# Bias rows built pair by pair on VectorE, two feature blocks side by side at the start of four layers, and fixed matmuls in nine waits of TensorE

## What is computed

```python
def first_block(...):                      # rows 0..271
    for i in range(2):
        a = rmsnorm(h, norm_mix_pre[i])
        m = forgetting_attention(a, ...) if i == 0 else gated_deltanet(a, ...)
        h = h + rmsnorm(m, norm_mix_post[i])
        f = conv_ffn(rmsnorm(h, norm_ffn_pre[i]), ...)
        h = h + rmsnorm(f, norm_ffn_post[i])
def second_block(...):                     # rows 16..271
    for layer in range(2):                 # MLA attention, then MoBA attention
        x = layer_norm(ALPHA * x + mixer(x, ...), ln_g[layer], ln_b[layer])
```

```python
logf = log_sigmoid(fl + b_forget); c = cumsum(logf, axis=1)
s = (q @ k.T) * 64 ** -0.5 + c_i[..., :, None] - c[:, :, None, :]
```

## Time and profile before

| | |
|---|---|
| time, median of 3 | 1306.91 us (1306.11 to 1307.09) |
| profiled execution, its own time | 1306.81 us |
| its span, first to last instruction | 1304.4 us |
| around the span | 2.4 us |
| busy: PE, DVE, ACT, POOL | 1198.2, 885.0, 714.1, 71.2 us |
| chain that ended last | PE 87%, DVE 7%, ACT 4%, issue 1% |
| mean granted clock of TensorE | 0.958 |

### The profile page before, as it was taken

One profiled execution on the slowest core, in us unless ns is written; L12 is line 12 of the kernel. 1 busy time (PEld: TensorE's weight loads), 2 busy tenths in 40 slices (PEclk: granted clock), 3 DMA queues, 4 the chain that ended last, 5 costly groups with the idle time before them and its releaser, 6 DMA issues.

```text
span 1304.4 us, 25965 instructions
## 1 busy us (share of the span) xinstructions
PE 1198.2 (92%) x9285; PEld 1120.2 (86%) x9285; DVE 885.0 (68%) x1676; ACT 714.1 (55%) x1478; POOL 71.2 (5%) x70
## 2 busy tenths in 40 slices
PE   5599997899999799988998889999978999799996
PEld 5588886899999699977996789999978999699995
DVE  4888875677764586866444468785456787768874
ACT  6477765566654368565224456665444555555543
POOL 0300000012100000002000001220000000000000
PEclk9799999899999899988997999999989999999999
DMA  6233324255555244530000426656634444334430
GB/s 240 93 108 118 120 90 129 66 177 176 174 165 166 88 160 152 157 122 2 2 2 1 129 66 190 181 170 185 177 107 123 137 128 135 129 122 141 141 113 33
DMA packets 49969, 160.22 MB, mean 123 GB/s; under 512 B 5488, under 2 KB 8432, under 8 KB 49776
## 3 DMA queue, kind: packets, MB, share of 16 engines
q1 hardware_dynamic: 49904, 159.35, 39.0%
HBM read 158.28 MB, written 1.05 MB: 122 GB/s over the span
## 4 chain that ended last, share of the span: by engine, by line
PE 87%; DVE 7%; ACT 4%; issue 1%; DMA 0%; SPq 0%; ACTq 0%; DVEq 0%
PE bank L360 23%; PE bank L362 21%; PE bank L361 21%; PE bank L418 4%; PE bank L1417 2%; PE bank L1425 2%; PE bank L862 2%; DVE rstd L435 2%; PE bank L842 1%; PE bank L827 1%; ACT w_hi L341 1%; DVE w_lo L346 1%; PE bank L1433 1%; PE bank L824 1%; DVE q_n L1091 1%
## 5 line engine op out<-in xcount | busy, mean ns | idle before, releaser
L360 PE MATMUL bank<-x_hi,w_hi 128*128 128x272 f32 (+2 forms) x1624 | 483.5, 298 | 44.5 <-DVE x_lo L463 28.8
L346 DVE TENSOR_TENSOR w_lo<-raw,w_hi 128x1024 fp32r<-128x1024 f32 (+5 forms) x332 | 370.6, 1122 | 214.2 <-ACT w_hi L341 213.5
L361 PE MATMUL bank<-x_lo,w_hi 128*128 128x272 f32 (+2 forms) x1624 | 468.4, 288 | 0.0
L362 PE MATMUL bank<-x_hi,w_lo 128*128 128x272 f32 (+2 forms) x1624 | 468.4, 288 | 0.0
L341 ACT ACTIVATE w_hi<-raw 128x1024 fp32r<-128x1024 f32 (+5 forms) x332 | 314.3, 955 | 95.3 <-PE bank L362 88.5
L360 PEld LDWEIGHTS bank<-x_hi,w_hi 128*128 128x128 f32 x1624 | 310.4, 191 | 64.5 <-issue 41.3
L361 PEld LDWEIGHTS bank<-x_lo,w_hi 128*128 128x128 f32 x1624 | 312.1, 192 | 0.2
L362 PEld LDWEIGHTS bank<-x_hi,w_lo 128*128 128x128 f32 x1624 | 311.6, 192 | 0.0
L360 PE MATMUL bank<-hid_hi,w_hi 128*128 128x272 f32 (+1 forms) x352 | 102.5, 291 | 0.0
L362 PE MATMUL bank<-hid_hi,w_lo 128*128 128x272 f32 (+1 forms) x352 | 100.5, 286 | 0.0
L361 PE MATMUL bank<-hid_lo,w_hi 128*128 128x272 f32 (+1 forms) x352 | 100.0, 284 | 0.0
(11 more groups left out here) (285 smaller groups left out, 1851.3 us busy)
## 6 DMA issues: line engine op xcount, KB each, us to landing
raw<-w_up SPq DMA_DIRECT2D x88, 512.0 KB, 3.9
raw<-w_attn SPq DMA_DIRECT2D x32, 512.0 KB, 4.6
raw<-w_dn SPq DMA_DIRECT2D x32, 512.0 KB, 4.3
raw<-w_moba SPq DMA_DIRECT2D x32, 512.0 KB, 3.9
raw<-w_down SPq DMA_DIRECT2D x32, 384.0 KB, 3.2
raw<-w_down SPq DMA_DIRECT2D x32, 320.0 KB, 3.2
raw<-w_mla SPq DMA_DIRECT2D x16, 384.0 KB, 3.3
raw<-w_attn_out SPq DMA_DIRECT2D x8, 512.0 KB, 4.3
```

Source lines behind the costliest of these rows:

```text
L346: nc.vector.tensor_tensor(w_lo[:, q, 0:wd], raw[:, q, 0:wd], w_hi[:, q, 0:wd].bitcast(F32), ALU.subtract).then_inc(lo_done, 1)
L360: nc.tensor.matmul(dst, hi, src[0][:, k, c0:c1], start=first, stop=False)
L361: nc.tensor.matmul(dst, hi, src[1][:, k, c0:c1], start=False, stop=False)
L362: return nc.tensor.matmul(dst, lo, src[0][:, k, c0:c1], start=False, stop=last)
```

## The change

Three edits, in one program.

1. `rows_a` has two rows, those of the next pair of heads. DVE makes them with two scalings of `c_2` by a head mask (`bias_rows(p)`), for every pair, between `norm_k(p)` and `outputs(p - 1)`. POOL's operation is gone. The work on `c_2` stands ahead of the three weight splits at the start of the first attention instead of behind them. `pe_scores` waits for `rows_ready` p + 1.
2. `two_products` runs slice k through the first and the second block before slice k + 1: FFN 0, FFN 1, the latent products and MoBA's queries and keys.
3. `keep_clock(n)` issues n matmuls of 256 columns from constants into bank 6, which nobody reads, with no wait: 36, 28, 32, 28, 36, 28, 38, 14 and 28 of them, 268 in all, ahead of sums of squares and ahead of layers' first blocks.

```diff
-            if f < 2:
-                pe.wait_ge((rows_ready, kr_ready)[f], 1 if f == 1 or isinstance(p, int) and p == 0 else 2)
+            if f == 0:
+                pe.wait_ge(rows_ready, p + 1)
+            if f == 1:
+                pe.wait_ge(kr_ready, 1)
...
+            def bias_rows(p):
+                if f == 0:
+                    st.settle()
+                    for hh in range(2):
+                        ins = nc.vector.tensor_scalar(rows_a[:, hh, :], c_2[:], tb("own_head_a")[:, bass.ds(p * 2 + hh, 1)], None,
+                                                      ALU.mult)
+                    ins.then_inc(rows_ready, 1)
...
+        def two_products(pe, name, dsts, cols, x_base):
+            for k in range(KT):
+                pe.wait_ge(x_ready, x_base + k + 1)
+                for q, dst in enumerate(dsts):
+                    if k == 0:
+                        weights_here(pe, name, 0, q)
+                    mm = product(dst, q, k * P, x_op, k, cols, k == 0, k == KT - 1)
+                    if k == KT - 1:
+                        mm.then_inc(chunk_used, 1)
...
+        def keep_clock(count):
+            for _ in range(count):
+                nc.tensor.matmul(bank[6][:, 0:2 * P], ones_r, fixed_r[:, 0:2 * P], start=True, stop=True)
...
             tail_pe(pe, 0, "w_attn_out", "post0", FULL, False)
+            keep_clock(36)
             sums_pe(pe, "pre1", KT, FULL)
+            keep_clock(28)
             ffn_pe(pe, 0)
+            keep_clock(32)
             sums_pe(pe, "pre2", KT, FULL)
+            keep_clock(28)
             pe.wait_ge(tables_in, 16)
             dn_pe(pe)
+            keep_clock(36)
             sums_pe(pe, "pre3", KT, TAIL)
+            keep_clock(28)
             ffn_pe(pe, 1)
+            keep_clock(38)
             latent_pe(pe)
             attention_pe(pe, 1)
             tail_pe(pe, 1, "w_mla_out", None, LAST, True)
+            keep_clock(14)
             sums_pe(pe, "var1", KT, LAST)
+            keep_clock(28)
             attention_pe(pe, 2)
...
-            pool.wait_ge(rows_ready, 1)
-            nc.gpsimd.tensor_tensor(rows_a[:, 2:16, :], c_2[:].unsqueeze(1).to_broadcast([P, 14, SC]),
-                                    tb("own_head_a")[:, 2:16].unsqueeze(2).to_broadcast([P, 14, SC]),
-                                    ALU.mult).then_inc(rows_ready, 1)
```

More of the change, by code:

```diff
@@ L257, in build @@
         SC = META + META + P + T
-        rows_a = put("rows_a", [16, SC], P, F32R)
+        rows_a = put("rows_a", [2, SC], P, F32R)
         c_2 = put("c_2", [SC])
@@ L817, in pe_scores @@
                 for hh in range(2):
-                    nc.tensor.matmul(bank[5 - hh][:, 0:SC], ones_r[:], rows_a[:, p * 2 + hh, :], start=True, stop=False)
+                    nc.tensor.matmul(bank[5 - hh][:, 0:SC], ones_r, rows_a[:, hh, :], start=True, stop=False)
             for b, ((q0, q1), (s0, s1)) in enumerate(part):
@@ L875, in step @@
                 queries, keys, sides, values, gates, turn_values = pe_project(pe, f, p, aw)
-                queries()
-                if not first:
-                    pe_scores(pe, f, p - 1)
-                keys()
+                if first and f == 2:
+                    pe.wait_ge(q_ready, 16)
+                    pe.wait_ge(k_ready, 16)
+                    two_products(pe, "w_moba", (bank[0][:, 0:SEQ], bank[1][:, 0:SEQ]), (META, T), X_BASE["ln1"])
+                else:
+                    queries()
+                    if not first:
+                        pe_scores(pe, f, p - 1)
+                    keys()
                 values()
@@ L1151, in splits @@
                     split_lo(dve, *following(name_of(f), p), q)
-            splits(0, (0, 1, 2))
             if f == 0:
-                z = sp_c[0:16]
+                z, full = sp_c[0:16], slice(SC - T, SC)
+                st(nc.vector.memset(c_2[:], 0.0))
                 dve.wait_ge(ln_done, 1)
@@ L1160, in attention_dve @@
                 st.settle()
-                st(nc.vector.memset(c_2[:], 0.0))
                 st(nc.vector.tensor_scalar(sp_b[0:16], z, -8.0, None, ALU.mult))
-                st.settle()
-                full = slice(SC - T, SC)
                 st(nc.vector.tensor_scalar(rows_a[0:16, 0, full], z, -8.0, None, ALU.mult))
@@ L1208, in ffn_pe, with unit @@
             name = f"w_up{f}"
-            def unit(u):
-                for r in range(2):
+            def unit(u, sides=(0, 1)):
+                for r in sides:
                     g = u * 2 + (r + FT * f)
@@ L1218, in unit @@
                         for k in range(KT):
-                            if isinstance(u, int) and u == 0 and q == 0:
-                                pe.wait_ge(x_ready, X_BASE[f"pre{2 * f + 1}"] + k + 1)
                             mm = product(bank[q][:, c0:c1], q, k * P, x_op, k, cols, k == 0, k == KT - 1)
                         mm.then_inc(chunk_used, 1)
-            unit(0)
+            if f:
+                pe.wait_ge(conv_done, FT * f)
+            two_products(pe, name, (bank[0][:, c0:c1], bank[1][:, c0:c1]), cols, X_BASE[f"pre{2 * f + 1}"])
+            unit(0, (1,))
             with pe.Fori(1, FT // 2) as u:
@@ L1361, in spread @@
                 wait(pe, dn["erow"], h)
-                nc.tensor.matmul(bank[4][:, 0:TP], sum_gc_r[:], rows_d[:, h, :], start=True, stop=True).then_inc(dn["row"], 1)
+                nc.tensor.matmul(bank[4][:, 0:TP], sum_gc_r, rows_d[:, h, :], start=True, stop=True).then_inc(dn["row"], 1)
             def turn_values(h):
@@ L1848, in latent_pe @@
             c0, c1 = META, T
-            for j in range(KT):
-                if j >= 2:
-                    pe.wait_ge(sq_ready, sq0["lat_q"] + j - 1)
+            two_products(pe, "w_latent", (bank[0][:, c0:c1], bank[1][:, c0:c1]), (c0, c1), X_BASE["post3"])
+            lat_sum(pe, 0)
+            for j in range(2, KT):
+                pe.wait_ge(sq_ready, sq0["lat_q"] + j - 1)
                 weights_here(pe, "w_latent", j // 4, j % 4)
                 for k in range(KT):
-                    if j == 0:
-                        pe.wait_ge(x_ready, X_BASE["post3"] + k + 1)
                     mm = product(bank[j % 2][:, c0:c1], j % 4, k * P, x_op, k, (c0, c1), k == 0, k == KT - 1)
                 mm.then_inc(chunk_used, 1)
-                if j:
-                    lat_sum(pe, j - 1)
+                lat_sum(pe, j - 1)
             lat_sum(pe, KT - 1)
@@ L1972, in constants_and_first_weight @@
                 act.wait_ge(s_in, 32)
-                nc.scalar.activation(ones_r[:], ones, ACT.Copy).then_inc(ones_ready, 1)
-                nc.scalar.activation(sum_gc_r[:], tb("sum_gc"), ACT.Copy).then_inc(ones_ready, 1)
+                nc.scalar.activation(ones_r, ones, ACT.Copy).then_inc(ones_ready, 1)
+                nc.scalar.activation(sum_gc_r, tb("sum_gc"), ACT.Copy).then_inc(ones_ready, 1)
                 prime(act, "pre0")
```

17 lines of the change are left out of this document (7 added, 10 removed).

## The result

| | before | after |
|---|---|---|
| time, median | 1306.5 us (1305.2 to 1307.1, 4 runs) | 1283.1 us (1281.6 to 1284.3, 4 runs) |
| profiled execution, its span | 1306.8, 1304.4 | 1281.6, 1279.6 |
| mean granted clock | 0.958 | 0.980 |

The ratio is 0.9825, 95% interval 0.9813 to 0.9837: 23.4 us less, where 23.4 less was forecast.

The account below looks back on a forecast made before the run. PE, 87% of the chain, was taken to bound the kernel by its own work, its waits and low-clock stretches. 1306.8 - 13.4 + 2.1 - 4.1 - 9.7 + 1.7 = 1283.4 us, range 1278.5 to 1292.

Parts of the forecast that it names:

- Part 1: First attention: q_n no longer held behind POOL's operation on rows_a, first biased scores at 43.5 instead of 56.92; 13.4 less.
- The price in the loop: First attention's pairs: scalings ahead of o_hi delay PE's scores, 0.25 in six pairs and 0.65 in the last; 2.1 more.
- PE's waits ahead of the looped scores: Sign of being right: a PE wait of 0.1 to 0.4 ahead of L824 in the looped pairs, some 1.5 in the last.
- Part 2: Sums of squares at layers' starts run at full clock behind fixed matmuls: post0 1.6, pre2 1.7, pre3 0.8; 4.1 less.
- Part 3: First two blocks side by side: FFN 0 2.55, FFN 1 2.4, MoBA 2.6, latent 2.1; 9.7 less.
- The 1.7 for a start lost to a swing: One of the eight starts and sums lost, with the clock low and the fill behind it late; 1.7 more.
- six matmuls at 0.125 keep up with a slice: FFN 0's paired blocks: six matmuls take 0.75, as much as the 0.76 between slices of x_lo.
- A: Rival: the clock falls in about half of the starts, half of parts 2 and 3 gone; 1292.6, or 1291; chance 0.20.
- B: Rival: the loop becomes DVE's, scalings at one element a cycle, 2.2 more than taken; 1285.6; chance 0.07.
- C: Rival: next weight chunks or ACT's second root are late, 6 to 8 of the 13.4 come back; 1290; chance 0.07.
- D: Rival: fixed matmuls run at the low level in all nine waits, parts 2 and 3 give nothing; 1314; chance 0.02.

Follow-up runs that it names:

- pool_late: Kernel before, with POOL's operation on the fourteen bias rows waiting until VectorE has made k_n of the first pair; 1308.45 us, ratio 1.0016.
- early_rows: Kernel after, with the two scalings in pairs 1 to 7 ahead of norm (of q), not behind norm (of k); 1281.86 us, ratio 0.9811.
- no_fills: Kernel after without any fixed matmul (every keep_clock left out); 1294.03 us, ratio 0.9908.
- one_block: Kernel after with the first blocks of the four layers one behind the other, fixed matmuls and bias rows kept; 1291.22 us, ratio 0.9892.
- spread_fills: more_fills with 3 fixed matmuls more between the heads of DeltaNet's spreading (six times); 1283.03 us, ratio 0.9824.
- more_fills: Kernel after with early_rows' order and 18 fixed matmuls each ahead of DeltaNet's spreading of roots and ahead of MLA; 1277.24 us, ratio 0.9783.
- dn_fills: spread_fills with fixed matmuls also in DeltaNet's waits for vb_all and, at the first level, d_tr; 1278.16 us, ratio 0.9795.
- best_fills: dn_fills without the three fixed matmuls between the heads of DeltaNet's spreading; 1271.68 us, ratio 0.9742.
- fills_plus: Kernel after with 14 fixed matmuls more in each of the nine waits; 1284.10 us, ratio 0.9830.
- bias_only: Kernel before with the bias-row edit alone, no fixed matmuls and no blocks side by side; 1293.95 us, ratio 0.9910.
- fills_half: Kernel after with half of the fixed matmuls in each wait; 1286.61 us, ratio 0.9857.
- sum_fills: Kernel after without the four fills of 28 behind the sums; 1287.54 us, ratio 0.9865.
- The square: Fixed matmuls and paired blocks, by ratio: neither (bias_only) 1294.7, blocks alone (no_fills) 1294.5, fixed matmuls alone (one_block) 1292.4, both (kernel after) 1283.6.

## Why the prediction was right, and where not

**Part 1, 13.4 less: right.** The first biased scores stand at 42.79, 13.48 less but for loads that ended 0.65 earlier in that execution. The steps were each right: wait of 1.41 (1.4), `q_n` in 0.50, no clock lost behind the wait. That POOL's operation was the cause of the slow `q_n` is shown by pool_late: moved by 4 us, it held up another operation until it ended. The stall followed POOL's operation and not `q_n`. The rule of the Trainium skill that the prediction named ("SBUF — State Buffer", section "Who interferes with whom") holds in that run (8.16 against 1.22). The stall is some 8 of the 13.4; the new order that the prediction worked out with it gave the rest.

**The price in the loop, 2.1: mis-sized, measured 1.09.** The period of the looped pairs grew by 0.1 and not by 0.25, and the last pair by 0.46 and not by 0.65; two scalings took 0.79, where I had 0.73. PE's waits ahead of the looped scores, forecast at 0.1 to 0.4, were at most 0.07. early_rows shows that it is the scalings' place that costs.

**Part 2, 4.1: 3.5 by the traces** (1.43, 1.52 and 0.56 for the sums where I said 1.6, 1.7 and 0.8; nothing at the layer norm, as said). 28 fixed matmuls took 3.71: 0.127 apart, not 0.119, which cost nothing, since all nine fills ended ahead of their data. Not all of the 3.5 needs a fill: in no_fills the sums of `pre2` gave 1.52 and those of `pre1` 0.89 too, because less of the low clock happened to fall on them.

**Part 3, 9.7: 9.5** (2.47, 2.31, 2.59, 2.17 for 2.55, 2.4, 2.6, 2.1).

**The number, 23.4 for 23.4: partly luck.** The terms of the traces are -13.5, +1.1, -3.5, -9.5 and +1.3, which is 24.1 less, with loads that ended 0.65 earlier 24.8. The loop was priced 1.0 too high, parts 2 and 3 together 0.8 too high, and these cancel in part; and the median lies 1.5 above the execution that was profiled.

**The 1.7 for a start lost to a swing: wrong in its place, nearly right in the sum.** One start of nine did lose the clock, but not one of those that I priced: DeltaNet's, where twelve matmuls at 0.125 fill 1.5 of 2.70 us. The two windows of the kernel after:

```profile
438.00:440.70 2.70, 2.28 (x12) 1.67 (x12) 2.70 (x8) 1.30 (x4) 0.00 (x0) 1.00 0.00 0
440.70:444.10 3.40, 3.27 (x14) 2.85 (x13) 2.75 (x7) 2.73 (x5) 0.00 (x0) 0.50 0.01 2
```

It cost nothing here: DeltaNet's first block took 6.81 in both kernels. In one_block, early_rows and spread_fills the clock fell some 4 us later, in the dense block behind it, and cost 1.5. In more_fills, dn_fills and best_fills it did not fall there at all. Yet early_rows, spread_fills and these three have the same matmuls in the same order up to that place. The windows over the second block, early_rows and then more_fills:

```profile
444.30:447.70 3.40, 3.40 (x16) 3.40 (x17) 3.37 (x4) 1.70 (x3) 0.00 (x0) 0.50 0.51 160
```

```profile
444.00:447.40 3.40, 3.40 (x27) 3.40 (x28) 3.37 (x4) 1.89 (x4) 0.00 (x0) 1.00 0.56 170
```

So the same instructions lose the clock in one execution and keep it in another, and a start lost or kept there is luck. The rule of the Trainium skill that I weighed ("TensorE: Matmul & The Clock Gate", section "A second HAM failure mode: psum-queue depth-cycling") fits that start in some traces, and no other in the kernel after: the paced sums and the paired slices, idle up to 40% or hardly at all, were granted 1.00 from 204 to 245. The rest of the 1.7 is 1.3 elsewhere: 0.45 in DeltaNet and 0.89 at MLA's start, behind a wait of 2.8 that was there before. There the kernel after was granted 0.69 over the first 9 us and the kernel before 0.81, with the same matmuls:

```profile
974.50:983.50 9.00, 8.90 (x55) 8.94 (x56) 5.76 (x12) 0.92 (x2) 0.00 (x0) 0.69 0.69 219
```

```profile
997.70:1006.70 9.00, 8.95 (x63) 8.98 (x64) 5.72 (x12) 1.74 (x5) 0.00 (x0) 0.81 0.70 219
```

With the same instructions at that place, fills_plus has 0.81 there again, and bias_only, one_block, fills_half and sum_fills don't have the 0.89 either, while no_fills and early_rows do. I take the 1.3 for chance, as at DeltaNet's start. In DeltaNet such a difference of 0.5 to 2 us came and went in nearly every kernel here.

**What the prediction did not price: parts 2 and 3 hang together.** It priced them apart and added them, 4.1 and 9.7. Together they did give nearly that. But its sentence that six matmuls at 0.125 keep up with a slice is true at full clock only, and by part 2 alone; at the low level they take 6 x 0.21 = 1.28 against 0.76. The square shows it: 0.2 and 2.3 alone, 11.1 together.

**The rivals.** A tied both parts to the clock and took a start where it falls as wholly lost, and half of the starts as such; no_fills keeps 0.8 to 1.0 of some 2.4 at each start without any fill, and one start of nine lost the clock. B (scalings too slow) did not come: two took 0.79. C (the next chunks or ACT's root late) did not come in the kernel after; in pool_late the stall did move, but by POOL's operation standing there still. D needed 1.25 of overrun in each wait; fills_plus had some 0.9 in each and lost 0.7 by ratio, so D was even further off than I said as long as the clock is up, and spread_fills shows what it is like when it isn't.

## What to carry to other kernels

A matmul stream whose waits are a few us long can lose time behind a wait as well as in it: filling the 2.8 us ahead of MLA made the blocks behind it 1.5 shorter than in the kernel before and 2.4 shorter than in the kernel after. Such a wait can be filled with matmuls that nobody needs, begun while the clock is up; those here ended 0.6 to 1.3 us before the data came. A small overrun was nearly free, while a fill that ran at the low clock, between work that had no such wait, took twice as long and was paid for in full. The traces of two kernels that differ by 1 to 2 us must be compared stage by stage, since the clock alone makes such a difference between executions. Price two edits that lift two limits of the same stretch together, and ask what each is worth without the other. A large operation of POOL is not free because POOL is idle: look at what DVE does with two inputs in SBUF while it runs, and move the work, not the time.

## What was not expected of the hardware

- Whether a wait brings the low clock varies at a given length. Five kernels with the same matmuls up to DeltaNet's second block made that block in 3.11 us (three of them) or 4.6 (two). A wait of 2.50 ahead of the same sixteen matmuls left them at 3.72 us or at 6.72; rests of 2.3 to 2.9 us in fills_half cost 1.45 at FFN 0, 1.05 at MoBA and nothing at FFN 1. The ten rests of 0.56 to 1.41 in the kernel after cost nothing at the sums and the paired starts.
- DVE's frozen operation is not slowed but stopped: `w_lo` took 8.16, which is its own 1.22 and 6.94 ahead of it, and these end within 0.13 of POOL's operation. The split that began 0.02 ahead of POOL's operation ran in its usual 1.22, and POOL's operation took 1.05 more.
- At full clock the fixed matmuls of 256 columns stand 0.125 to 0.127 apart, no closer than real ones of 272 with weights that change (0.125).
